# A decoder block rewritten without stage barriers: attention set between the merge-gate matmuls, token-major V, out and FF2, modulation on column strips

## What is computed

```python
mod = silu(c) @ w_ada + b_ada           # (B, 6*4096): shift1, scale1, gate1, shift2, scale2, gate2
h = rmsnorm(x) * (1 + scale1) + shift1
proj = h @ w_in                         # NSA q, k/v, gates | FoX q, k, v, forget | merge gates
o_nsa = compressed + selected-block + sliding-window attention, gated (16 heads, 4 kv groups)
o_fox = softmax attention with a cumulative log-forget bias (16 heads)
y = sigmoid(g_a) * (o_nsa @ w_up_a) + sigmoid(g_b) * (o_fox @ w_up_b)
x = x + gate1 * (y @ w_out)
h2 = rmsnorm(x) * (1 + scale2) + shift2
x = x + gate2 * (relu(h2 @ w_ff1)**2 @ w_ff2)      # w_ff1 4096 x 16384
```

## Time and profile before

| | us |
|---|---|
| median of 3 runs (11374.79 to 11425.48) | 11375.37 |
| the profiled execution | 11369.84 |
| its span on the slowest core, core 1 | 11368.1 |
| PE busy in it | 9271.7 (82%) |
| ACT, DVE, POOL busy | 1783.1, 1449.0, 558.1 |

### The profile page before, as it was taken

How to read it: one execution, slowest core, us unless ns; L and a number is a source line. 1 busy time by engine, 2 the same in 40 slices (tenths; PEclk the granted TensorE clock), 3 DMA queues, 4 the chain that set the end, 5 groups by cost and what they waited for, 6 DMA issues and landing times.

```text
span 11368.1 us, 128077 instructions; the slowest of 8 cores (11333.8 to 11368.1 us)
## 1 busy us (share of the span) xinstructions
PE 9271.7 (82%) x49482; PEld 4380.2 (39%) x49482; DVE 1449.0 (13%) x3744; ACT 1783.1 (16%) x3025; POOL 558.1 (5%) x830
## 2 busy tenths in 40 slices
PE   1168866888899986656666799969999999999998
PEld 1133332333344444422222344434444444444444
DVE  0011022110000001122232211020000001000000
ACT  0121121112200005522222100020000000000000
POOL 1000000000000000000000020000000000000000
PEclk9989988999999997755555699979999999999999
DMA  9843433333344449943333366544564564465455
GB/s 141 146 92 74 78 94 72 70 67 76 76 90 96 95 85 146 147 74 54 59 54 58 60 115 127 127 114 77 122 131 77 102 132 94 81 132 115 77 117 116
DMA packets 818947, 1097.09 MB, mean 97 GB/s; under 512 B 152496, under 2 KB 734512, under 8 KB 751792
## 3 DMA queue, kind: packets, MB, share of 16 engines
q0 software_dynamic: 301600, 759.01, 40.8%
q1 hardware_dynamic: 516752, 329.89, 10.2%
HBM read 1709.32 MB, written 138.41 MB: 163 GB/s over the span
## 4 chain that ended last, share of the span: by engine, by line
PE 78%; DMA 7%; ACT 5%; DVE 5%; issue 3%; SPq 1%; DVEq 0%; ACTq 0%; POOL 0%; POOLq 0%
PE ps L239 75%; DMA ws_55<-w_ada 4%; PE ps L242 2%; ACT tn_255 L245 1%; DMA fv_157<-d_fv 1%; SPq L268 1%; DVEq L128 0%; DMA fv_159<-d_fv 0%; ACT hT L245 0%; DVE oaccS L258 0%; DVE oaccS L252 0%; DMA fv_158<-d_fv 0%; DMA xt_243<-out 0%; DMA xt_104<-xc 0%; DMA xq_256<-out 0%
## 5 line engine op out<-in xcount | busy, mean ns | idle before, releaser
L239 PE MATMUL ps<-hT,ws_56 128*128 128x512 bf16 x2752 | 622.3, 388 | 21.4 <-DMA ws_56<-w_in 20.9
L239 PE MATMUL ps<-hT,ws_53 128*128 128x512 bf16 (+1 forms) x2688 | 598.9, 384 | 21.3 <-DMA ws_53<-w_in 19.9
L239 PE MATMUL ps<-hT,ws_55 128*128 128x512 bf16 x2688 | 599.7, 385 | 0.8
L239 PE MATMUL ps<-hT,ws_54 128*128 128x512 bf16 x2688 | 597.5, 384 | 1.2
L239 PE MATMUL ps<-hT,ws_52 128*128 128x512 bf16 (+1 forms) x2688 | 595.5, 383 | 1.6 <-DVE yb_129 L258 0.5
L239 PE MATMUL ps<-oT,ws_56 128*128 128x512 bf16 x2080 | 457.0, 380 | 17.3 <-DMA ws_56<-w_ff 17.3
L245 ACT ACTIVATE tn_255<-ps,modT 128x512 f32<-128x512 f32 x256 | 175.9, 687 | 1867.5 <-PE ps L242 1834.4
L239 PE MATMUL ps<-oT,ws_55 128*128 128x512 bf16 x2080 | 458.5, 381 | 8.8 <-DMA ws_55<-w_upa 8.8
L239 PE MATMUL ps<-oT,ws_54 128*128 128x512 bf16 x2048 | 449.4, 380 | 0.0
L239 PE MATMUL ps<-oT,ws_53 128*128 128x512 bf16 x2016 | 443.9, 381 | 0.0
L239 PE MATMUL ps<-oT,ws_52 128*128 128x512 bf16 x2016 | 441.3, 379 | 0.0
(11 more groups left out here) (580 smaller groups left out, 9517.7 us busy)
## 6 DMA issues: line engine op xcount, KB each, us to landing
out<-xr_258 SPq DMA_DIRECT2D x256, 256.0 KB, 3.4
ws_56<-w_ff POOLq DMA_DIRECT2D x52, 1024.0 KB, 8.5
ws_52<-w_ff POOLq DMA_DIRECT2D x51, 1024.0 KB, 8.6
ws_53<-w_ff POOLq DMA_DIRECT2D x51, 1024.0 KB, 8.4
ws_54<-w_ff POOLq DMA_DIRECT2D x51, 1024.0 KB, 8.5
ws_55<-w_ff POOLq DMA_DIRECT2D x51, 1024.0 KB, 8.3
ws_56<-w_in POOLq DMA_DIRECT2D x43, 1024.0 KB, 8.3
ws_54<-w_in POOLq DMA_DIRECT2D x42, 1024.0 KB, 8.2
```

What stands on the lines that cost most here:

```text
L239: S.emit(PE, lambda e: e.matmul(out_, lhsT, rhs, start=start, stop=stop, skip_group_check=True), reads, writes)
```

## The change

The program is written anew. What it does, in the order of the code:

- **Recorder.** Semaphores count only instructions that someone waits for; no barriers. A tile's memory may be given to another tile, whose first writer then waits for the old one's users. The order of all weight loads is found by a first pass, and `Slots` issues the next load as soon as a slot is given back: four slots, three in the attention stretch, six in the MLP. All weights are laid out as 128 rows of 4096 columns.
- **Fill.** `tick(ns)` counts the GEMM time emitted (426 ns for two matmuls); generators started by `spawn` are continued when their due time is passed. Epilogues, the context build, background modulation and attention are such generators.
- **Modulation** (`mod_tile`): silu(c) is the stationary operand, 32 columns wide, and 512 columns of w_ada move; four column strips of the array take different rows of w_ada, and a small fp32 matmul adds them up. Tiles 0 to 15 come first, with the build of own tokens beside; 16 to 38 beside the context projections, 39 to 47 beside attention. Gate tiles are kept as rows in memory (`d_gate`).
- **Projections.** Own FoX and NSA queries first, with the context build beside them; then keys and the compression inputs for both halves (128 matmuls for a load); then V by `gemm_t`, which has tokens as stationary operand and 512 weight columns moving, so the result is token-major.
- **Attention and merge gates.** FoX, then NSA run as one generator beside the 64 merge-gate blocks. Steps ask for `FILL` = 690 ns of GEMM between them. FoX takes one head at a time and two query tiles in one bank; NSA keeps two heads in a bank and does the four heads' divisions in one instruction. Sigmoid becomes Tanh with a DVE step.
- **Out and FF2** by `gemm_t`, with gate and residual on DVE, no transposes in FF2; out's epilogue also transposes the new x in bf16 and sums its squares, and `norm2` then modulates in place.

```diff
-            for j in range(4):
-                for k in range(8):
-                    mm(bank.t[:, j:j + 1], wv[:, k, j * 128:(j + 1) * 128], silu.t[:, s_ * 8 + k, 0:1],
-                       s_ == 0 and j == 0 and k == 0, s_ == 3 and k == 7, [w.b, silu.b], [bank.b])
...
+            for i in range(2):
+                for j in range(4):
+                    k = 2 * j + i
+                    mm(bank.t[32 * j:32 * j + 32, 0:512], silu.t[:, 8 * s + k, :], w.t[:, 512 * k:512 * k + 512],
+                       s == 0 and i == 0, s == 3 and i == 1, [w.b, silu.b], [bank.b])
+            slots.put(w)
+            yield "piece"
+        cp(DVE, rows.t[:], bank.t[:], [], [rows.b, bank.b])
+        yield "rows"
...
+    def tick(ns):
+        st["gemm"] += ns
+        while tasks and tasks[0][0] <= st["gemm"]:
+            step_task()
...
+    def gemm_f(src, ncol, places, ring, epilogue, kcs=range(32)):
...
+        for tb, t0, idx in places:
+            p = ring.next()
+            for n, kc in enumerate(kcs):
+                mm(p.t[0:ncol, 0:512], wv[:, kc, :], tb.t[:, kc, t0:t0 + 512], n == 0, n == 31,
+                   [w.b, rb(tb, kc, t0 // 512)], [p.b])
+                if n % 2:
+                    tick(426)
+            spawn(epilogue(p, idx))
+        slots.put(w)
...
+    def gemm_t(srcs, places, ring, epilogue):
...
+        last = [(ring.next(), pl) for pl in places[-4:]]
+        for kc in range(32):
+            for p, (tb, t0, idx) in last:
+                one(p, tb, t0, kc)
+            tick(852)
+            if kc % 8 == 7:
+                slots.put(ws[kc // 8])
+        for p, (tb, t0, idx) in last:
+            spawn(epilogue(p, idx))
...
+            act(sq.t[:], p.t[:], AF.Square, [], [sq.b, p.b])
+            yield 1300
+            mm(px.t[:], onesb, sq.t[:], True, True, [sq.b, cb.b], [px.b])
+            act(rs.t[:], px.t[:], AF.Ln, [epsc.b], [rs.b, px.b], scale=1.0 / 128, bias=epsc.t[:, 0:1])
...
+    def mod_bg():
+        for t in range(16, 48):
+            for what in mod_tile(t, PS[7], PS[7]):
+                yield {"piece": 9000, "rows": 1500, "done": 500}[what]
...
+                    for f in pend:
+                        pv4(*f)
+                    pend = [(pT, vs.t[:, kt, 0:129], vs.b, kt == 0, kt == qc)]
+                    yield FILL
...
+    spawn(attention())
+    for ci in range(64):
+        gemm_f(("inF", F_MG + ci), 128, own_places(ci), Rmg, epi_merge)
+    drain(True)
...
-                    for j in range(4):
-                        tr(pz.t[:, j * 128:(j + 1) * 128], tmp.t[:, j * 128:(j + 1) * 128], identf, [tmp.b, cf.b],
-                           [pz.b])
...
+                tt(DVE, nw.t[:], p.t[:], g.t[:], ALU.mult, [g.b], [nw.b, p.b])
+                tt(DVE, nw.t[:], nw.t[:], pv_.t[:], ALU.add, [pv_.b], [nw.b])
```

More of the change, by code:

```diff
@@ L30, in __init__, with live @@
         self.w = None
         self.r = {}
-class Sem:
-    __slots__ = ("h", "val")
-    def __init__(self, h):
-        self.h = h
-        self.val = 0
+        self.inh = list(inh)
+        self.dead = False
+    def live(self):
+        assert not self.dead, "use of a tile whose memory was given away"
+        if self.inh:
+            inh, self.inh = self.inh, []
+            for o in inh:
+                if not o.dead:
+                    o.live()
+                o.dead = True
+                for x in ([o.w] if o.w is not None else []) + list(o.r.values()):
+                    k = id(x) if x.dma else x.q.name
+                    if k not in self.r or self.r[k].idx < x.idx:
+                        self.r[k] = x
@@ new lines, in at @@
+        self.n += 1
+        t = self.nc.alloc_sbuf_tensor_at(f"{name}_{self.n}", list(shape), dtype, offset=off)
+        step = per // nsub
+        self.live = [x for x in self.live if not x[2].dead]
+        bs = []
+        for i in range(nsub):
+            lo, hi = off + i * step, off + (i + 1) * step
+            bs.append(Buf([b for (l, h, b) in self.live if l < hi and lo < h]))
+        self.live += [(off + i * step, off + (i + 1) * step, b) for i, b in enumerate(bs)]
+        return TB(t, bs)
@@ new lines, in emit_program @@
+    slots = Slots(issue, order)
+    slots.free = [wslot(o_w + 8192 * i) for i in range(4)]
+    slot3 = slots.free[3]
+    cb = P.tile("cb", [128, NCB], BF16)
+    cf = P.tile("cf", [128, NCF], F32)
+    modT = P.tile("modT", [128, 192], F32, nsub=48)
+    badaT = P.tile("badaT", [128, 192], F32)
+    gT = P.tile("gT", [128, 64], F32)
+    s1T = P.tile("s1T", [128, 32], F32, nsub=8)
+    s2T = P.tile("s2T", [128, 32], F32)
+    qkg = P.tile("qkg", [128, 4], F32)
+    bfgn = P.tile("bfgn", [16, 1], F32)
@@ L1062, in build_program @@
[L1062 to L1067 removed]
+    dma(SP, bfgn.t[:], bfg_d, [], [bfgn.b])
+    dma(POOL, cb.t[:], cb_d, [], [cb.b])
+    act(csig.t[:], cTf.t[:], AF.Sigmoid, [cTf.b], [csig.b])
+    tt(DVE, csig.t[:], cTf.t[:], csig.t[:], ALU.mult, [cTf.b], [csig.b])
@@ new lines, in emit_program @@
+    drain()
+    def mod_bg():
+        for t in range(16, 48):
+            for what in mod_tile(t, PS[7], PS[7]):
+                yield {"piece": 9000, "rows": 1500, "done": 500}[what]
+                while st["hold"]:
+                    yield 3000
+        stt(s2T.t[:], modT.t[:, 128:160], 1.0, gT.t[:, 32:64], ALU.add, ALU.mult, [modT.bs[b] for b in range(32, 40)] +
+            [gT.b], [s2T.b])
+    spawn(mod_bg(), keep=True)
+    Z = Bump(M, o_kv, o_end)
+    lspT = Z.tile("lspT", [128, 16, 16], F32)
@@ new lines, in emit_program, with epi @@
+    pre = Pre(load_x, [(nb, i) for nb in range(8) for i in range(8)], 2)
+    gate_load(0, 0)
+    for nb in range(8):
+        if nb < 7:
+            gate_load(0, nb + 1)
+        g = gcur[nb % 2]
+        def epi(p, i, nb=nb, g=g):
+            yield from epi_out(p, (nb, i, g, pre.get(8 * nb + i)))
+            if nb == 7 and i in (3, 7):
+                spawn(norm2(i // 4), 200)
+        gemm_t([("out", 4 * nb + s) for s in range(4)], [(yT, 128 * i, i) for i in range(8)], Rt, epi)
+    tick(0)
@@ L1068, in build_program @@
+    if order is None:
+        return slots.asked
+    assert slots.asked == slots.order
+    S.finish([b for row in g_out for b in row])
+    return None
+def build_program():
+    order = emit_program(bass.Bass("TRN2", target_bir_lowering=False), None)
+    nc = bass.Bass("TRN2", target_bir_lowering=False)
+    emit_program(nc, order)
     return nc
```

1859 lines of the change are left out of this document (971 added, 888 removed).

## The result

The changed kernel takes 9690 to 9694 us where the kernel before takes 11,368 to 11,425: a ratio of **0.851, 95% interval 0.847 to 0.855**. The forecast was 9170, a ratio of 0.806; the sign and the range (8740 to 9800) held, the point was 520 us low. In some executions of either kernel one die runs at a lower clock; they are left out of every comparison here, which is why the times above lie under the median of all four, 9872.

The account below looks back on a forecast made before the run. The prediction took dense matmuls (7334 us of the 11,368 us span) as fixed and 4034 us as overhead to cut. It summed 7320 dense, 572 attention matmuls, 465 start and smaller terms to 9170 us, range 8740 to 9800.

Parts of the forecast that it names:

- The dense price: All projections and MLP: 0.2158 us for a matmul of 512 columns, 7320 us for 33,920 of them.
- The Trainium skill's rule: GEMMs: the die falls to 13/16 of the clock once three cores run dense matmuls; an estimated +1.8 ms.
- The start: Modulation before the first projection, with the own build beside it: 465 us (440 to 560), paced by loads.
- NSA's chains: NSA: three DVE chains stop PE in each of 32 rounds; about 2 us left of each, 190 us in all.
- FoX 90: FoX: waits for two exps between scores and values, some 0.2 us in 416 steps, 90 us.
- Strips: Background modulation on four column strips: 120 us, between 55 (four at once) and 221 (one by one).
- Second build: Own projections: the context build runs beside 2048 matmuls (442 us) and its loads are covered.
- The 55 us for norm epilogues: Projections: waits left for epilogue squares at 160 places, 55 us of the 530 before.
- Context projections: Context projections with the compression: 1095 us by the prediction's terms dealt out to this stretch.
- The clock term: Attention beside the merge gates: 5% of 1.8 ms for a clock of 0.95, 90 us, nothing elsewhere.
- attention's latency stays: Rival: fills come too late, so FoX and NSA keep their PE idle time; 9780 us, chance 0.14.
- more is hidden than I think: Rival: strips at 55, start at 440, attention waits at 100, V and out waits gone; 8730 us, chance 0.09.

Follow-up runs that it names:

- the new deal: Changed kernel with NSA's merge-gate work dealt otherwise, 480 ns between score tiles and 1500 or 2100 at the chains, same sum per round: 9534 us, single execution.
- the 128 rows: Changed kernel with the 400 selection matmuls of NSA on all 128 rows (96 of them zeros) in place of 32: 9553 and 9571 us, ratio 0.8411.
- the last kernel: Changed kernel plus eight edits: chunks, rotation tables and query tiles loaded ahead, compression phases apart, 128-row selection, merge work redealt, four x1 and four xr buffers: 9152 us.
- the query loads: Query tile pairs loaded one tile ahead in NSA, run with four residual buffers on top of the five edits (9215 us): 9199 us, ratio 0.8081.

## Why the prediction was right, and where it was not

**Right, by its own steps.** The dense price held where hardly anything else stands: up and MLP, 18,432 of the 33,920 matmuls, came within 1 us each of what it gave, at 1.00, without fp32 transposes. The Trainium skill's rule that the prediction weighed there ("TensorE: Matmul & The Clock Gate", Part 1) again did not show in the executions compared here: 3560 us of MLP at 1.00 on all eight cores. The start came to 476 us for 465, at 185 GB/s and a share of 1.01, as the new load shape was read from the earlier trace rows. The slot waits at V's block starts are 5.2 us each (31.2 in 6) for 4 to 5 forecast. NSA's chains leave 2.3, 2.1 and, with `sc`, 1.8 us of waiting a round for a forecast of 2. All waits of the attention stretch come to some 309 us for 290 (FoX 90, NSA 190, tail 10), but in FoX that is partly luck: the exps, for which the 90 us were meant, cost 27, and a wait that had no term, for `of` at the output transposes, 42.

**Strips: right mechanism, term too large.** 120 us was the middle between 55 and 221. Four strips run at once: 128 groups of 0.65 us, with the changes of tile shape on both sides, are 83.

**Second build: the step that failed most by one cause (+174; +151 on cores 0 and 4).** It said that the context build's loads "need about 300 us of full DMA share in that time, so it is covered". That is a sum of bandwidth, and the bandwidth was there (share 0.53). What was not covered is the latency of each load on two engines that work in order: 5 to 6 us from issue to landing (the medians of the two buffers), asked for at the moment of use, 64 times, with the epilogues' squares behind it. Asked for two steps earlier, the stretch takes 516 us for a forecast of 499. The 55 us for norm epilogues, with its condition "unless ACT is at a context square", looked at ScalarE's work, 1.06 us for such a square, and not at what that work waits for.

**Context projections (+101).** Two things had no term. The rotation table, a load for each place into one buffer: 45 us of the stretch. And the 64 compression matmuls stood in "288 sum, rotation and compression matmuls, 62 us" at the dense price, 14 us for them; they took 59, by the stride. With both gone the stretch is 1103 us for 1095.

**Attention (+193).** The 400 selection matmuls were counted among "1120 of 512 columns, 242" at the dense price. The prediction did say of the strips that the change of tile shape "has no price in this trace"; it did not ask where else the shape changes. That is 80 us, and 119 with the clock it costs. The clock term was 90 us, from the 0.95 of an earlier stretch; 0.94 of 2072 us is 124 us. That makes some 114 of 193 for these two, and the waits above the 290 forecast add 19. The other 60 us were not parted further. The 1800 to 1900 us at 0.95 that were named as the sign did not come; with the new deal, which won 147 us in NSA from waits and clock alone, and the 128 rows the stretch is in that range (1825 us in the last kernel, which has other edits too).

**The rivals.** The likeliest bracket, 8800 to 9450 with a chance of 0.70, was missed. The time lies in the bracket of "attention's latency stays" (9450 to 9850), yet not by its mechanism: the attention waits add up to what was forecast. The high bound 9800 was taken for that latency, so it is partly luck that the range holds the time. The terms that "more is hidden than I think" names add up to about 8810, not 8730; the time is far from both. The rivals asked whether the large things hide each other; what came in between were small ones that no line of the sum named. With eight edits against them the program takes 9152 us, 18 under the forecast of 9170 for a program without them. That nearness is partly chance: the new deal and the query loads also took off waits that the forecast had allowed for.

## What to carry to other kernels

When work is set beside a GEMM, ask of each load in it when it is issued and who stands in order behind the instruction that waits for it; enough bandwidth doesn't cover a load that is asked for at its use. Price a matmul by its operand's stride and by whether its rows or columns of the array differ from its neighbours', not by its length alone; where an operand of 32 rows can be padded with zeros to 128, try it: here the full one was cheaper. Where a burst of n epilogues passes several rings, count the buffers of each: here four were needed in both, and widening one only moved the wait to the other.

## What the runs showed of the hardware

- A matmul over 32 or over 64 rows between matmuls over 128 costs about 0.1 us on the way in and 0.1 on the way out at the upper clock (0.31 and 0.32 us against 0.2158); the same operands padded to 128 rows cost nothing extra, and a matmul over 127 rows between such ones doesn't either (0.22 and 0.22).
- A moving operand that takes every 16th bf16 element costs 0.92 us for 508 columns against 0.22. A ScalarE copy that writes with a step of 256 bytes takes 2.45 us for 128 x 512 against 0.60.
- Eight 32 x 512 matmuls on four column strips hold TensorE for 0.55 us at the upper clock, on one strip for 1.84; the step into the four strips from a matmul over 128 columns costs another 0.1 (0.31 against 0.2158).
- The granted clock fell with the holes in TensorE's work: NSA, with the same attention matmuls, had 0.53 alone, 0.92 beside the merge GEMM, and 0.98 when that GEMM was dealt to where the chains are.
